# All four modulation rows ahead of the first product, and another order of loads, in an attention layer's opening

## The reference, cut to what matters

```python
mod = s_c @ w_ada[layer] + b_ada[layer]
shift, scale, gate = mod[:, None, :D], mod[:, None, D:2 * D], mod[:, None, 2 * D:]
mod_c = s_cc @ w_ada[layer] + b_ada[layer]
u_lat = _rmsnorm(h_lat, norm_g[layer]) * (1.0 + scale) + shift
u_ctx = _rmsnorm(h_ctx, norm_g[layer]) * (1.0 + mod_c[D:2 * D]) + mod_c[:D]
...
z = u_lat @ w_in
```

## Time and profile before

| | |
|---|---|
| median of 3 runs | 2407.82 us (2406.93 to 2407.83) |
| profiled execution | 2405.5 us, its span 2403.7 us |
| TensorE busy | 2265.1 us, 94% of the span |
| VectorE, ScalarE, GpSimd busy | 1509.5, 1189.7, 517.2 us |
| mean granted clock of TensorE | 0.98 |
| prologue, to the loop's first product | 118.1 us, TensorE busy in some 76 of it |

### The profile page before, as it was taken

One profiled execution on the slowest core, in us unless ns is written; L12 is line 12 of the kernel. 1 busy time (PEld: TensorE's weight loads), 2 busy tenths in 40 slices (PEclk: granted clock), 3 DMA queues, 4 the chain that ended last, 5 costly groups with the idle time before them and its releaser, 6 DMA issues. The chain is left out here.

```text
span 2403.7 us, 33934 instructions
## 1 busy us (share of the span) xinstructions
PE 2265.1 (94%) x12000; PEld 1962.9 (82%) x12000; DVE 1509.5 (63%) x2386; ACT 1189.7 (49%) x1720; POOL 517.2 (22%) x299
## 2 busy tenths in 40 slices
PE   5899999999999999999997999799999999995998
PEld 3688888888888888888885888688988899894887
DVE  3476575765757657576586436557766776677444
ACT  3444434444344443444434334366777677767322
POOL 1123132231323323233230300022212221220300
PEclk8999999999999999999998999899999999997999
DMA  7012111211112111121106555111111111113654
GB/s 282 27 46 66 55 57 33 84 60 55 57 38 83 56 55 57 42 85 50 55 27 223 164 166 177 50 44 53 53 45 61 53 53 51 55 53 137 222 154 144
DMA packets 165398, 200.04 MB, mean 83 GB/s; under 512 B 51080, under 2 KB 125960, under 8 KB 162184
## 3 DMA queue, kind: packets, MB, share of 16 engines
q1 hardware_dynamic: 155320, 174.53, 23.0%
q10 hardware_dynamic: 9792, 23.07, 2.7%
q0 software_dynamic: 144, 0.52, 0.1%
HBM read 166.11 MB, written 31.98 MB: 82 GB/s over the span
## 5 line engine op out<-in xcount | busy, mean ns | idle before, releaser
L944 PE MATMUL ps<-u_hi,w_hi 128*128 128x512 f32 (+1 forms) x1464 | 533.4, 364 | 0.0
L944 PE MATMUL ps<-u_hi,w_lo 128*128 128x512 f32 (+1 forms) x1464 | 519.3, 355 | 0.0
L944 PE MATMUL ps<-u_lo,w_hi 128*128 128x512 f32 (+1 forms) x1464 | 518.2, 354 | 0.0
L944 PEld LDWEIGHTS ps<-u_hi,w_lo 128*128 128x128 f32 x1464 | 276.7, 189 | 40.0
L944 PEld LDWEIGHTS ps<-u_lo,w_hi 128*128 128x128 f32 x1464 | 277.4, 190 | 35.3
L944 PEld LDWEIGHTS ps<-u_hi,w_hi 128*128 128x128 f32 x1464 | 277.0, 189 | 35.3
L1616 POOL TENSOR_TENSOR o_w_lo<-o_w_raw,o_w_hi 128x1024 fp32r<-128x1024 f32 x48 | 139.1, 2898 | 670.2 <-ACT o_w_hi L1631 670.2
L1886 PE MATMUL ps<-u_hi,o_w_hi 128*128 128x426 f32 (+2 forms) x640 | 238.3, 372 | 14.0 <-POOL o_w_lo L1616 9.3
L574 ACT ACTIVATE probs<-probs,neg_max 128x640 f32<-128x640 f32 (+1 forms) x160 | 122.9, 768 | 250.1 <-DVE neg_max L777 249.0
L467 POOL TENSOR_TENSOR w_lo<-w_stage,w_hi 128x1024 fp32r<-128x1024 f32 x63 | 151.1, 2400 | 411.7 <-ACT w_hi L527 411.7
L1886 PE MATMUL ps<-u_hi,o_w_lo 128*128 128x426 f32 (+2 forms) x640 | 237.8, 372 | 0.0
(11 more groups left out here) (190 smaller groups left out, 4401.2 us busy)
## 6 DMA issues: line engine op xcount, KB each, us to landing
y_tile<-y_scratch SPq DMA_DIRECT2D x72, 512.0 KB, 5.1
w_stage<-in_w_even SPq DMA_DIRECT2D x63, 512.0 KB, 3.6
o_w_raw<-in_w_odd SPq DMA_DIRECT2D x48, 512.0 KB, 3.6
ada_piece<-in_w_ada SPq DMA_DIRECT2D x18, 1024.0 KB, 5.6
wout_raw<-in_w_out SPq DMA_DIRECT2D x16, 1024.0 KB, 9.4
y_scratch<-h_backward SPq DMA_DIRECT2D x16, 512.0 KB, 2.7
ada_piece<-in_w_ada SPq DMA_DIRECT2D x3, 2048.0 KB, 13.5
h_scratch<-h_tile ACTq DMA_DIRECT2D x18, 256.0 KB, 2.3
```

Source lines behind the costliest of these rows:

```text
L944: last = nc.tensor.matmul(ps[:, bank(j, g), 0:t - f], w[:, slot, c * P:(c + 1) * P], x[:, c, f:t], start=(c == 0 and n == 0), stop=(c == K ...
```

## The change

**Loads.** x pairs 0 and 1 and the two W come first, then piece 0, the small biases, piece 2 (in two halves, as piece 3), V's W, piece 1, piece 3; the rest as before.

**TensorE.** The first three transposes of group 0 come first, then all four rows with their columns, then group 0 unbroken: Q and K of 8 chunks, V of 8 chunks. Group 2's transposes begin under V of group 1 at chunk 3 and come in every chunk from there (five under V, three under K).

**ScalarE.** Squares four tiles and takes one root for them, splits W, then the row copies with V's high half between, then `u_hi` of group 0 with the squares of tiles 4 to 7 in between. It scales tiles 6 and 7 itself.

**VectorE.** One inverse for tiles 0 to 3 and four scalings, the low halves of the three W (`split_w`), both `mod_half`, then groups 0, 1 and 2 unbroken, with the scalings between the groups. GpSimd no longer works on W in the prologue.

```diff
@@ -238,10 +238,11 @@
     x_loaded = [sem(f"x_loaded{i}") for i in range(NT // 2)]
-    ada0_loaded = [sem(f"ada0_loaded{i}") for i in range(5)]
+    ada0_loaded = [sem(f"ada0_loaded{i}") for i in range(6)]
...
 sem("eps_set"), sem("squared"), sem("root_done"), sem("rinv_done"), sem("x_scaled"))
+    rinv_ready, x_scaled_act = sem("rinv_ready"), sem("x_scaled_by_act")
@@ -394,16 +395,17 @@
         sp.dma_start(k["ident"][:], a["ident"]).then_inc(c_loaded, 16)
-        load_mod(0)
         load_pair(0)
-        for name in ("bada", "normg"):
-            sp.dma_start(k[name][:], a[name]).then_inc(bias_loaded, 16)
-        load_mod(2)
...
         load(1, 1)
+        load_mod(0)
+        for name in ("bada", "normg"):
+            sp.dma_start(k[name][:], a[name]).then_inc(bias_loaded, 16)
+        for h in range(2):
+            sp.dma_start(ada0[2][:, h, :], a["w_ada"][2, h]).then_inc(ada0_loaded[2 + 3 * h], 16)
+        sp.dma_start(v_raw[:], a["w_even"][2]).then_inc(v_loaded, 16)
         load_mod(1)
-        sp.dma_start(v_raw[:], a["w_even"][2]).then_inc(v_loaded, 16)
@@ -486,11 +488,7 @@
     def prologue():
-        split_lo(0, 0)
-        split_lo(1, 1)
         nc.gpsimd.memset(toe[:], 0.0).then_inc(zeros_set, 1)
-        pool.wait_ge(w_hi, 3)
-        nc.gpsimd.tensor_tensor(v_lo_w[:], v_raw[:], v_hi_w[:].bitcast(F32), ALU.subtract).then_inc(w_lo, 1)
@@ -601,9 +599,10 @@
-    def root(q):
-        act.wait_ge(squared, 2 * q + 2)
-        nc.scalar.activation(rms[:, 2 * q:2 * q + 2], ss[:, 2 * q:2 * q + 2], ACT.Sqrt, scale=1.0 / D,
+    def root(q, pairs):
+        r = slice(2 * q, 2 * (q + pairs))
+        act.wait_ge(squared, r.stop)
+        nc.scalar.activation(rms[:, r], ss[:, r], ACT.Sqrt, scale=1.0 / D,
@@ -636,33 +635,32 @@
         act.wait_ge(eps_set, 1)
-        copy_row(0)
-        square(0)
-        square(1)
-        root(0)
-        copy_row(1)
-        square(2)
-        square(3)
-        root(1)
+        for t in range(4):
+            square(t)
+        root(0, 2)
...
         split_hi(0, 1)
-        for c in range(3):
-            u_hi(0, c)
-        copy_row(2)
-        u_hi(0, 3)
+        copy_row(0)
+        copy_row(1)
...
         nc.scalar.activation(v_hi_w[:], v_raw[:], ACT.Copy).then_inc(w_hi, 1)
+        copy_row(2)
         copy_row(3)
+        for c in range(4):
+            u_hi(0, c)
+        square(4)
         u_hi(0, 4)
+        square(5)
+        root(2, 1)
         u_hi(0, 5)
-        square(4)
+        square(6)
         u_hi(0, 6)
-        square(5)
-        root(2)
+        square(7)
+        root(3, 1)
         u_hi(0, 7)
-        square(6)
-        square(7)
-        root(3)
+        act.wait_ge(rinv_ready, 1)
+        for t in (6, 7):
+            nc.scalar.activation(x[:, t, :], x[:, t, :], ACT.Copy, scale=rinv[:, t:t + 1]).then_inc(x_scaled_act, 1)
@@ -673,7 +671,7 @@
         square(9)
-        root(4)
+        root(4, 1)
@@ -847,23 +845,32 @@
-    def scale_rows(q, link):
-        r = slice(2 * q, 2 * q + 2)
-        dve.wait_ge(root_done, q + 1)
+    def inverse(r, link):
...
         link(nc.vector.tensor_scalar(ss[:, r], ss[:, r], -0.5, 1.5, ALU.mult, ALU.add))
-        link(nc.vector.tensor_tensor(rinv[:, r], ss[:, r], rms[:, r], ALU.mult))
-        for t in (2 * q, 2 * q + 1):
+        return nc.vector.tensor_tensor(rinv[:, r], ss[:, r], rms[:, r], ALU.mult)
+    def scale_rows(n, r, link):
+        dve.wait_ge(root_done, n)
+        link(inverse(r, link))
+        for t in range(r.start, r.stop):
...
+    def split_w(c):
+        hi, lo, raw = (whi[:, c, :], wlo[:, c, :], stage[:, c, :]) if c < 2 else (v_hi_w[:], v_lo_w[:], v_raw[:])
+        dve.wait_ge(w_hi, c + 1)
+        nc.vector.tensor_tensor(lo, raw, hi.bitcast(F32), ALU.subtract).then_inc(w_lo, 1)
...
-        dve.wait_ge(mod0_turned, 2 * h + 2)
+        dve.wait_ge(mod0_turned, 4)
@@ -911,17 +918,18 @@
         link = Link(dve, rinv_done)
-        scale_rows(0, link)
+        scale_rows(1, slice(0, 4), link)
+        split_w(0)
+        split_w(1)
+        split_w(2)
         mod_half(0, link)
-        scale_rows(1, link)
-        split_chunks(0, 0, 4)
         mod_half(1, link)
-        split_chunks(0, 4, KC)
-        scale_rows(2, link)
-        scale_rows(3, link)
-        split_chunks(1, 0, 4)
-        scale_rows(4, link)
-        split_chunks(1, 4, KC)
+        split_chunks(0, 0, KC)
+        scale_rows(2, slice(4, 6), link)
+        dve.wait_ge(root_done, 3)
+        inverse(slice(6, 8), link).then_inc(rinv_ready, 1)
+        split_chunks(1, 0, KC)
+        scale_rows(4, slice(8, 10), link)
@@ -1005,8 +1013,10 @@
         for c in range(KC):
-            if c == 0 or (j == 3 and c == 4):
-                pe.wait_ge(ada0_loaded[j + c // 4], 16)
+            if c == 0:
+                pe.wait_ge(ada0_loaded[j], 16)
+            if c == 4 and j >= 2:
+                pe.wait_ge(ada0_loaded[{2: 5, 3: 4}[j]], 16)
@@ -1027,7 +1037,9 @@
         if c == 0:
-            pe.wait_ge(x_scaled, tiles(g)[-1] + 1)
+            pe.wait_ge(x_scaled, (4, 6, 8)[g])
+            if g == 1:
+                pe.wait_ge(x_scaled_act, 2)
@@ -1057,29 +1069,17 @@
         pe.wait_ge(silu_done, 4)
-        mod_row(0)
-        mod_columns(0)
-        mod_row(1)
-        mod_columns(1)
...
             turn_x(0, c)
-        for c in range(4):
+        for n in range(4):
+            mod_row(n)
+            mod_columns(n)
+        for c in range(KC):
...
             first(CK, 0, c)
-            turn_x(0, c + 3)
-            if c == 1:
-                mod_row(2)
-                mod_columns(2)
-        for c in range(4):
-            first(CV, 0, c)
-        mod_row(3)
-        mod_columns(3)
-        for c in range(4, KC):
-            first(CQ, 0, c)
-            first(CK, 0, c)
-            if c == 4:
-                turn_x(0, 7)
-        for c in range(4, KC):
+            if c + 3 < KC:
+                turn_x(0, c + 3)
+        for c in range(KC):
@@ -1090,12 +1090,12 @@
             first(CV, 1, c)
-            if c in (1, 3, 5):
-                turn_x(2, c // 2)
+            if c >= 3:
+                turn_x(2, c - 3)
...
             first(CK, 2, c)
-            if c + 3 < KC:
-                turn_x(2, c + 3)
+            if c + 5 < KC:
+                turn_x(2, c + 5)
...
                 first(j, 2, c)
```

## The result

| | before | changed |
|---|---|---|
| median | 2407.82 us (2406.93 to 2408.66) | 2388.78 us (2388.53 to 2389.56) |
| profiled execution | 2405.5 us | 2388.96 us |
| its span | 2403.7 us | 2387.2 us |
| start to the first pass's `q_stack` | 119.68 us | 105.93 us |
| from there to the eighth pass's | 1048.94 us | 1047.12 us |

The ratio of the times is 0.9922, 95% interval [0.9904, 0.9939]. The table says where to look, `q_stack` being the first VectorE instruction of a pass: the opening gave 13.75 us, about as forecast; 1.82 us come from the loop and 0.93 us from what follows, neither of which the diff touches; and 2.5 us are in no row of it, since the profiled execution before lay 2.3 us under its median and the one after 0.2 us over its own.

A forecast was written before the change was run, and what follows sets the result against it. The order of the chain before the loop, with TensorE waiting almost only for VectorE, was taken as the bound. -10.6 (to group 1's first product), -1.9 (group 1) and -0.6 (group 2) gave -13.1 us: median 2394.7 us, range 2391.5 to 2402.0.

The forecast's parts named there:

- The walk through the opening: Step-by-step timing of everything before the loop's first pass; claimed -13.1 us in sum, itself off by 2 us either way.
- A: The first `u_hi` of group 0, at 33.36 us before; forecast at 37.0 us, 3.6 us later.
- B: The first matrix product of group 1, at 76.95 us before; forecast at 66.3 us, -10.6 us.
- C: The end of the K product of group 2, at 109.95 us before; forecast at about 97 us.
- Stays up: Four rows on TensorE: the clock, risen inside row 0, stays high across gaps of 0.77 us, giving A = 37.0 us; chance 0.50.
- Rival 1: The clock falls in the row stage: each row up to 2.6 us longer, A at most 44.3, 2402.0 us; chance 0.38.
- The half speed in group 0: Start of group 0's product after TensorE's idle time: 4.8 us at half speed were assumed.
- the 1.0 us taken back: Group 2: GpSimd's mask addition (1.16 us) may lie over the last two `u_lo`, taking 1.0 of the 1.6 us gain.
- it does not look at the clock on the wall, so I carry a gain here to the end at its full size: The loop after the opening: its first pass starts when the opening is done, so the whole -13.1 us reaches the end.
- 2392.4 us for a profile, 2394.7 us for the median: Whole program: forecast totals with -13.1 us, from 2405.5 us for the profiled execution and 2407.8 for the median before.
- Rivals 2 and 3: 2: clock low through group 0 too, 2414.8 us, chance 0.04; 3: gain not carried into the loop, 2405 to 2408, 0.08.

## Why the prediction was wrong

**The walk through the opening was right.** In the order of its steps:

| step | forecast, us | measured, us |
|---|---|---|
| x scaled, transposes start | 17.75 | 17.69 |
| row 0 ends | 23.1 | 23.0 |
| rows 1, 2, 3 end | 26.8, 30.6, 34.7 | 26.6, 30.6, 34.6 |
| A | 37.0 | 36.91 |
| first product | 40.3 | 40.06 |
| Q and K of group 0 end | 58.1 | 58.46 |
| B | 66.3 | 66.93 |
| Q and K of group 1, length | 16.4 | 16.40 |
| C | 96.7 | 96.07 |
| loop's first product | about 105 | 104.37 |
| change of the opening | -13.1 | -13.75 |

"Stays up" held for the clock between rows: in the row stage 12.65 of 16.50 us were work, with four gaps of 0.72 us; the column says 1.00, and rows 1 to 3 have the lengths of the high level (row 0, at 2.59 us, not yet). Rival 1 fell with it. The Trainium skill's rule on psum-queue depth-cycling (TensorE: Matmul & The Clock Gate), by which this rival's time would have come, finds no support here: the row stage has just such small idles between groups of matmuls, and the rows stay at 1.92 us. One number of the walk was taken wrongly: 3 MB between 9.57 and 17.33 us are 2.59 us per MB; the 2.54 come from V's W (7.5 MB between 9.57 and 28.6 us). It did no harm: the rows that wait for pieces 1 and 3 go on at 28.66 and 33.56 us, where 28.6 and 33.7 were forecast. The half speed in group 0 took 5.6 us where I had 4.8 (0.55 as the mean of two levels over 6.27 us, so nine tenths of it low).

**One term was mis-sized: the 1.0 us taken back** for GpSimd's mask addition over the last two `u_lo`. It starts at 95.52 us, when they are done:

```profile
94.78 0.75 DVE L898 TENSOR_TENSOR u_lo<-x_mod,u_hi 128x256 fp32r<-128x256 f32 x2
...
95.52 1.16 POOL L479 TENSOR_TENSOR bias_piece<-bias_piece,row_mask 128x576 f32<-128x576 f32 x1
```

The memset ahead of it (93.06 to 95.45) left VectorE alone. Without the term the forecast is -14.1 us, 0.35 too much: group 0 ended 0.6 us later than forecast, groups 1 and 2 took 0.3 us less, and the way from C to the first pass 0.1 us more.

**The step that failed is the last one, the way from the opening to the median.** First, "it does not look at the clock on the wall, so I carry a gain here to the end at its full size". It doesn't, but it depends on how many instructions VectorE has ahead of it: 1.8 us that had nothing to do with the order of the opening, and that came back when four idle memsets restored the number. No row of before says that five instructions fewer remove a gap, but the gap itself was in the trace, an idle 0.29 us with no other engine in it, with TensorE waiting behind it, and I looked at no row of the loop. Second, "2392.4 us for a profile, 2394.7 us for the median": I added the 2.3 us between profile and median of before to the changed kernel as if they were a constant. The changed kernel's two offsets are -0.2 and 0.9 us. By the estimate above 1.6 us of the missing 2.5 are openings of the kernel before in which the clock was low for longer than in its first profile; this is not tested. The 0.9 us at the end, and the 0.9 of the 2.5 that the mean end accounts for, remain open. The range had only the walk's own error on its lower side, so nothing of this fitted into it.

**Rivals 2 and 3** did not occur: group 0 was at the high clock from 46.33 us on, and the first pass came 13.75 us earlier, so the gain was carried.

## What to carry to other kernels

Putting all small dependent work (the four rows) ahead of a ring of chunks pays although the first chunk starts later, as long as the data for it lands early: here each without the other lost 9.6 of 13.75 us. Of an edit ahead of a loop, ask also what else it shifts: compare one pass of the loop in both traces, and see which of its new or missing idles another engine waits behind, before the difference of two medians is put down to the edit. And an offset between a profile and a median is to be carried to the changed kernel only if what makes it is still there.

## What the hardware showed that I had not expected

- A pause of some 0.3 to 0.4 us that belongs to certain numbers in VectorE's instruction stream (192, 320, 448 seen), in every pass of a loop. The number of instructions ahead of the loop decides which instruction meets it. With 130 ahead TensorE waits behind one of the two, and the loop is 1.8 to 2.2 us of 2400 longer; with 122, 125, 133 and 141 it is not.
- The same opening with its first product at full rate in two profiles and low until 40 us in two others, and ends of it from 119.55 to 124.19 us; idle matmuls that fill the pause ahead of a product kept the clock at 1.00 and took 1.9 us off the opening.
- A VectorE operation on 128x4 numbers took 2.34 us beside a subtraction on GpSimd.
